# Two halves of a sample's expert lookup: where the dot products and the weighted sums stand between the u and the v stage

## The reference, cut to what matters

```
s        = einsum('thpc,hpkc->thpk', q, keys)            # 8 heads, 2 halves, 128 keys
v1, i1   = top_k(s[:, :, 0], 16);  v2, i2 = top_k(s[:, :, 1], 16)
vals, sel = top_k(v1[..., None] + v2[..., None, :], 16)   # 16 of 16384 experts per head
eid      = e1 * 128 + e2
gate     = softmax(vals)
act      = gelu(einsum('thkd,td->thk', u[eid], h))        # dot products
y        = einsum('thk,thkd->td', gate * act, v[eid])     # weighted sums
```

## Time and profile before

| | |
|---|---|
| median of 3 runs | 2619.02 us (2616.82 to 2620.7) |
| profiled execution | 2623.06 us, of which the span from first to last instruction is 2621.3 us |
| PE busy | 2351.1 us (90%) |
| DVE busy | 1774.2 us (68%) |
| ACT busy | 1396.8 us (53%) |
| POOL busy | 175.5 us (7%) |
| granted TensorE clock, mean | 0.935 |

### The profile page before, as it was taken

How to read it: one execution, slowest core, us unless ns; L and a number is a source line. 1 busy time by engine, 2 the same in 40 slices (tenths; PEclk the granted TensorE clock), 3 DMA queues, 4 the chain that set the end, 5 groups by cost and what they waited for, 6 DMA issues and landing times.

```text
span 2621.3 us, 55587 instructions
## 1 busy us (share of the span) xinstructions
PE 2351.1 (90%) x18004; PEld 2208.7 (84%) x18004; DVE 1774.2 (68%) x4136; ACT 1396.8 (53%) x2867; POOL 175.5 (7%) x185
## 2 busy tenths in 40 slices
PE   6996799999887799999897996899999976999996
PEld 3963699999885599999797875799998966999995
DVE  2435538888757777756555877568888789777654
ACT  2511356666558855555455222466666589555553
POOL 1000000000300012100000000000002200211000
PEclk7985799999999999999988877899999999999998
DMA  7453436555964578855543112346557810887552
GB/s 255 162 171 136 143 129 213 178 184 196 335 208 165 187 234 272 280 178 183 170 136 121 49 56 80 131 156 196 179 182 272 300 45 9 273 276 254 184 184 82
DMA packets 126860, 468.34 MB, mean 179 GB/s; under 512 B 14417, under 2 KB 14577, under 8 KB 125633
## 3 DMA queue, kind: packets, MB, share of 16 engines
q1 hardware_dynamic: 103104, 375.44, 41.7%
q0 software_dynamic: 23680, 92.01, 11.2%
HBM read 456.74 MB, written 10.65 MB: 178 GB/s over the span
## 4 chain that ended last, share of the span: by engine, by line
PE 74%; DVE 9%; ACT 7%; DMA 6%; issue 3%; ACTq 1%; SPq 0%; POOL 0%; DVEq 0%; POOLq 0%
PE ps L1275 21%; PE ps L1276 21%; PE ps L1277 21%; ACT hs L568 5%; DMA big<-in_u_rows,choice 4%; DMA raw<-in_ada_w 2%; PE ps L1304 2%; PE ps L1421 1%; DVE spl L715 1%; PE ps L1437 1%; DVE big L1122 1%; PE ps L1450 1%; ACT hs L581 1%; PE ps L1518 1%; PE ps L1340 1%
## 5 line engine op out<-in xcount | busy, mean ns | idle before, releaser
L1275 PE MATMUL ps<-hs,spl 128*128 128x256 f32 (+1 forms) x4960 | 1425.9, 287 | 88.0 <-DVE hs L767 46.0
L1276 PE MATMUL ps<-hs,spl 128*128 128x256 f32 (+1 forms) x4960 | 1425.9, 287 | 0.0
L1277 PE MATMUL ps<-hs,spl 128*128 128x256 f32 (+1 forms) x4960 | 1421.3, 287 | 0.0
L715 DVE TENSOR_TENSOR spl<-raw,spl 128x512 fp32r<-128x512 f32 x1240 | 839.4, 689 | 554.7 <-ACT spl L449 551.0
L449 ACT ACTIVATE spl<-raw 128x512 fp32r<-128x512 f32 x1240 | 772.4, 630 | 522.8 <-PE ps L1277 522.3
L1275 PEld LDWEIGHTS ps<-hs,spl 128*128 128x128 f32 x4960 | 953.2, 192 | 99.4 <-issue 58.4
L1276 PEld LDWEIGHTS ps<-hs,spl 128*128 128x128 f32 x4960 | 951.8, 192 | 0.0
L1277 PEld LDWEIGHTS ps<-hs,spl 128*128 128x128 f32 x4960 | 948.0, 191 | 0.0
L1518 PE MATMUL ps<-hs,onehot 128*128 128x128 f32 x1024 | 154.5, 298 | 71.7 <-ACT hs L581 61.3
L1518 PEld LDWEIGHTS ps<-hs,onehot 128*128 128x128 f32 x1024 | 131.1, 201 | 100.1 <-ACT hs L581 92.3
L551 ACT ACTIVATE big<-ps 128x256 f32 (+1 forms) x256 | 98.4, 384 | 139.3 <-PE ps L1277 137.8
(11 more groups left out here) (242 smaller groups left out, 1464.9 us busy)
## 6 DMA issues: line engine op xcount, KB each, us to landing
raw<-in_peer_u SPq DMA_DIRECT2D x256, 512.0 KB, 3.7
raw<-in_peer_v SPq DMA_DIRECT2D x256, 512.0 KB, 3.5
raw<-in_ada_w SPq DMA_DIRECT2D x96, 512.0 KB, 5.0
raw<-in_peer_wq SPq DMA_DIRECT2D x32, 512.0 KB, 3.4
raw<-in_hg_w_in SPq DMA_DIRECT2D x32, 512.0 KB, 3.5
raw<-in_ab_w_in SPq DMA_DIRECT2D x28, 512.0 KB, 3.5
raw<-in_ab_w_out SPq DMA_DIRECT2D x8, 512.0 KB, 4.0
big<-in_state_hgrn POOLq DMA_DIRECT2D x8, 512.0 KB, 3.9
```

The source lines that it names most:

```text
L715: dve.tensor_tensor(spl[:, slot % 2, 1, cols], raw[:, slot, cols], spl[:, slot % 2, 0, cols].bitcast(F32), ALU.subtract).then_inc(low_read ...
L1275: pe.matmul(out, spl[:, slot, 0, cols], high, start=start, stop=False, skip_group_check=True)
L1276: pe.matmul(out, spl[:, slot, 0, cols], low, start=False, stop=False, skip_group_check=True)
L1277: return pe.matmul(out, spl[:, slot, 1, cols], high, start=False, stop=stop, skip_group_check=True)
```

## The change

The 32 dot products are divided: the first 16 (EARLY) stay behind the top-k search in the u stage, the other 16 go into groups 0 to 7 of the v stage, one after every second block, at the places where sums stood. The 32 sums move from groups 0 to 15 to groups 10 to 25 (SUM_FROM = 10). With them move their v lookups, the Gelu of the dot products (ACT, now between groups 8 and 9 of the v stage), the multiplication with the softmax gate (DVE, now ahead of group 10), PE's fold (now ahead of group 27) and the read-back of x behind the last v lookup. A dot product in the u stage now brings exactly two feeds. PACE goes from 1450 to 1420.

```
-PACE = 1450
+PACE = 1420
+EARLY = 16
+SUM_FROM = 10
...                                             (ACT, u stage)
-                act.wait_ge(dot_done, PICKS * (l + 1))
-                act.activation(samp_w, samp_w, ACT.Gelu).then_inc(samp_gelu, 1)
...                                             (ACT, v stage)
-                section(act, f"v{l}", expert_out)
+                section(act, f"v{l}", expert_out, groups=(0, SUM_FROM - 1))
+                act.wait_ge(dot_done, PICKS * (l + 1))
+                act.activation(samp_w, samp_w, ACT.Gelu).then_inc(samp_gelu, 1)
+                section(act, f"v{l}", expert_out, groups=(SUM_FROM - 1, EXP // 4))
...                                             (DVE)
+            def dot(l, j):
+                dve.wait_ge(u_landed[j % U_SLOTS], landed(l, j, U_SLOTS))
+                row = fetched[:, j % U_SLOTS, :]
+                dve.tensor_tensor_reduce(row, row, h_rows, 1.0, 0.0, ALU.mult, ALU.add, samp_w[:, j:j + 1]).then_inc(dot_done, 1)
...                                             (DVE, behind the top-k search)
-                for j in range(PICKS):
-                    dve.wait_ge(u_landed[j % U_SLOTS], landed(l, j, U_SLOTS))
-                    row = fetched[:, j % U_SLOTS, :]
-                    dve.tensor_tensor_reduce(row, row, h_rows, ...).then_inc(dot_done, 1)
-                    spent(1230)
+                for j in range(EARLY):
+                    dot(l, j)
+                    spent(2 * PACE)
...                                             (DVE, v stage)
-                dve.wait_ge(samp_gelu, l + 1)
-                link(dve.tensor_tensor(samp_w, samp_w, samp_gate, ALU.mult))
...
-                section(dve, f"v{l}", with_sample, first=True, groups=(0, PICKS // V_SLOTS))
-                section(dve, f"v{l}", expert_out, groups=(PICKS // V_SLOTS, EXP // 4))
+                late = (PICKS - EARLY) // 2
+                for i in range(late):
+                    for s in range(4):
+                        expert_out(i, s)
+                        if s % 2:
+                            dot(l, EARLY + 2 * i + s // 2)
+                section(dve, f"v{l}", expert_out, groups=(late, SUM_FROM))
+                dve.wait_ge(samp_gelu, l + 1)
+                link(dve.tensor_tensor(samp_w, samp_w, samp_gate, ALU.mult))
+                sum_to = SUM_FROM + PICKS // V_SLOTS
+                section(dve, f"v{l}", with_sum, first=True, groups=(SUM_FROM, sum_to))
+                section(dve, f"v{l}", expert_out, groups=(sum_to, EXP // 4))
...                                             (PE, v stage)
-                middle = PICKS // V_SLOTS + 1
+                middle = SUM_FROM + PICKS // V_SLOTS + 1
```

More of the change, by code:

```diff
@@ L1118, in topk @@
                 picked = False
-                for j in range(PICKS):
-                    dve.wait_ge(u_landed[j % U_SLOTS], landed(l, j, U_SLOTS))
-                    row = fetched[:, j % U_SLOTS, :]
-                    dve.tensor_tensor_reduce(row, row, h_rows, 1.0, 0.0, ALU.mult, ALU.add, samp_w[:, j:j + 1]).then_inc(dot_done, 1)
-                    spent(1230)
+                for j in range(EARLY):
+                    dot(l, j)
+                    spent(2 * PACE)
                     if not picked and fed[0] >= topk_row + 4:
@@ L1210, in expert_out, with with_sum @@
                         weight_low(i * 4 + (s + 1), (s + 1) % 2)
-                def with_sample(i, s):
+                def with_sum(i, s):
                     expert_out(i, s)
@@ L1215, in with_sample @@
                         slot = s // 2
-                        dve.wait_ge(v_landed[slot], i * 16 + 16 * (PICKS // V_SLOTS * l + 1))
-                        w = choice[:, 1, bass.ds(i * 2 + (T_PROMPT + slot), 1)]
-                        if isinstance(i, int) and i == 0 and slot == 0:
+                        dve.wait_ge(v_landed[slot], i * 16 + 16 * (PICKS // V_SLOTS * l + 1 - SUM_FROM))
+                        w = choice[:, 1, bass.ds(i * 2 + (T_PROMPT + slot - 2 * SUM_FROM), 1)]
+                        if isinstance(i, int) and slot == 0:
                             ins = dve.tensor_scalar(samp_sum, fetched[:, slot, :], w, None, ALU.mult)
                         else:
-                            dve.wait_ge(sum_done, i * 2 + (PICKS * l + slot))
+                            dve.wait_ge(sum_done, i * 2 + (PICKS * l + slot - 2 * SUM_FROM))
                             ins = dve.scalar_tensor_tensor(out=samp_sum, in0=fetched[:, slot, :], scalar=w, in1=samp_sum, op0=ALU.mult, op1=ALU.add)
                         ins.then_inc(sum_done, 1)
-                section(dve, f"v{l}", with_sample, first=True, groups=(0, PICKS // V_SLOTS))
-                section(dve, f"v{l}", expert_out, groups=(PICKS // V_SLOTS, EXP // 4))
+                late = (PICKS - EARLY) // 2
[10 more added lines that the diff above has]
+                section(dve, f"v{l}", expert_out, groups=(sum_to, EXP // 4))
                 dve.wait_ge(half_done, 2 * (SPLIT[f"v{l}"] + EXP))
```

## The result

The changed kernel takes 2592.96 us in the median of six runs (2585.57 to 2598.87), against 2622.0 us (2616.82 to 2633.19) for the kernel before: ratio 0.9874, 95% interval 0.985 to 0.9898. Forecast were 2591.5 us and a range of 2585 to 2603. The profiled execution took 2592.62 us, 30.4 less than the profiled one before.

What follows compares the result with a forecast made beforehand. PE's matmul pace bounds the kernel, with lookup rounds through three slots stalling it in the dot stretches. 2623.06 - 30.1 + 0.6 = 2593.6 us for the profiled execution; 2591.5 us forecast as a middle with 2589.5, range 2585 to 2603.

Steps and rivals of the forecast that it cites:

- The stall and its size: Dot stretches of both u stages: PE loses 16.3 and 13.8 us to late lookups, together 30.1 us, all of it returning.
- further margin: u stage: beyond 5.8 us of cover left, transfers come at a lower rate than the earlier 319 to 321 GB/s.
- the three longest parts: Lookup round in u: longest dot product, POOL issue and landing come to 11.4 us, against 17.16 us of cover.
- The clock share: Dot stretches: 9.1 of the 30.1 us are matmuls at lower clock behind waits, counted as returning with the idle time.
- The rival (only 21.0 us): Dot stretches: dips have another cause than waits, so only idle time returns, 2600.6 us; chance 0.10.
- The v stage at 0: v stages: sixteen added dot products each and sums moved to groups 10 to 25 cost PE 0.
- Gelu, fold, read-back at 0: v stage: moving Gelu, fold and read-back costs 0; table loads for Gelu would cost at most 2.6 us in all.
- Remains of 0.3 us per layer: Top-k stretch: allowance for remains such as the softmax behind a dot product, 0.6 us in the sum.
- its 1.1 us: Top-k stretch: PE waits only 1.1 us, so PACE 1420 changes between -1.1 and +1.1 per layer, taken as 0.
- The middle between 2589.5 and 2593.6: Whole call: the profile's 4.04 us over the median lie in vanishing waits (2593.6) or elsewhere (2589.5); middle 2591.5 us.

Runs made afterwards that it cites:

- one block per dot product: The changed kernel with one block instead of two behind each of the 16 dot products of the u stage: 2597.63 us, ratio 0.9895.
- the v half alone: Kernel before with Gelu, gate multiplication, v lookups and sums moved to v groups 10 to 25; all 32 dot products stay in u, PACE 1450: 2618.65 us, ratio 0.998.
- three groups of runs: The changed kernel, unaltered, run in three groups, each beside the kernel before: medians 2592.96, 2590.82 and 2593.71 us.
- the run with unwaited lookups: Kernel before, lookups 2 to 32 into slots 0 and 1, dot products reading h_rows and waiting for the first lookup alone: 2592.71 us, ratio 0.9888.
- the one-slot kernel: The changed kernel with one slot for u lookups instead of three: 2627.95 us, ratio 1.0017 to the kernel before.

## Why the prediction was right

**The stall and its size.** Right in both layers: 16.3 and 13.8 us from counting matmuls, 16.6 and 13.9 measured on the u stages. The lookups' round was the cause, as taken from the chain. Without the wait, with DVE's work unchanged and nearly the same traffic, the gain is the same, and three, two and one slots and one block per dot product behave as round against cover says.

The agreement to 0.3 us is partly made: both numbers come from the same profile of the kernel before. In the profile of the v half alone the same stall of layer 1 made a u stage of 385.1 us, which is 20.9 us over the changed kernel's 364.2 and not 13.9. What supports the sum beyond that profile are the medians, which lie 29.0, 30.6 and 31.2 us apart in the three groups of runs.

The prediction named the lower rate of transfers as further margin. It brought the lookups of the u stage nothing: they land in 6.9 us where it was 7.0, and the spacing alone covers them. Also, POOL's issue lies within the landing: in the earlier trace rows the dot product (1.23), 0.28 us and the landing (8.35) make up the round of 9.88. So the 11.4 us of the three longest parts count the issue twice, on the safe side.

**The clock share.** The 9.1 us beyond idle time came back: the two u stages are 30.5 us shorter, 9.5 more than the idle time of 21.0. The rival (only 21.0 us) would have left some 2600.6 us and a clock under 1.00 in the dot stretch; the profile shows 1.00. That the dips follow the waits and not the traffic is shown by the run with unwaited lookups: nearly the same GB/s, no waits, clock 1.00. In that point the rival's own argument was half right: waits do not always bring a dip. One block per dot product had 2.8 and 3.0 us of waits in the two layers, none over 1.1, and full clock. In the one-slot kernel the clock fell to 0.66 behind a wait of 1.8 us, and stayed at 1.00 behind its longest, 2.7 us (between 675 and 685). The slice with the first, and the next two:

```profile
655.00:660.00 5.00, 3.19 (x28) 2.98 (x26) 2.42 (x5) 2.74 (x6) 0.42 (x1) 1.00 0.47 153
660.00:665.00 5.00, 5.00 (x29) 5.00 (x30) 2.28 (x4) 0.89 (x2) 0.73 (x1) 0.66 0.71 216
665.00:670.00 5.00, 5.00 (x45) 5.00 (x43) 2.48 (x5) 4.54 (x7) 1.15 (x1) 1.00 0.64 206
```

The Trainium skill, "TensorE: Matmul & The Clock Gate", section on HAM oscillation, says that waits for DMA that let the clock fall pay the slower clock again each time. The trace agrees for this stall: 9.5 us came back beyond the idle time. But these two kernels show waits that let no clock fall, and in the one-slot kernel the longer wait is one of them, so here the length of a wait did not tell.

**The v stage at 0.** Right. The v half alone measures 0.998 (0.9956 to 1.0005). Layer 1's v stage is 1.4 us longer in the profile after. The rows put that at its start, where the clock is low before the stage's first dot product begins (2195.28): the one-block kernel, with the same v stage, has 364.9 us as before. The first windows of the two, the changed kernel first:

```profile
2185.00:2190.00 5.00, 2.97 (x21) 2.81 (x22) 4.25 (x10) 2.19 (x5) 0.00 (x0) 0.92 0.00 0
2190.00:2195.00 5.00, 5.00 (x34) 5.00 (x34) 1.86 (x5) 1.57 (x3) 0.00 (x0) 0.74 0.30 107
```

```profile
2189.00:2194.00 5.00, 2.97 (x26) 2.81 (x25) 4.29 (x11) 1.77 (x5) 0.00 (x0) 1.00 0.00 0
2194.00:2199.00 5.00, 5.00 (x44) 5.00 (x44) 3.35 (x7) 2.52 (x5) 0.06 (x1) 1.00 0.40 120
```

PE is busy 2.97 us in both first slices, and yet 34 matmuls follow in one and 44 in the other. Whether the change makes such a start more likely stays open: in layer 1 five of the eight profiles with dot products in the v stage have it, all three of the changed kernel among them, and none of the three profiles without. In layer 0 the kernel before has it as well (clock 0.71 from 925 to 930). The prediction also says that groups 10 to 25 held no sums before; groups 10 to 15 did, under the same load per group.

**Gelu, fold, read-back at 0.** Right; no table load came with the Gelu, and the read-back landed in 7.8 to 8.0 us.

**Remains of 0.3 us per layer.** Slightly too much: from 645 to 753 the profile after shows no wait of PE on DVE at all. The top-k stretch keeps its 1.1 us, as assumed.

**The middle between 2589.5 and 2593.6.** A choice between two readings of the profiled run's 4 us, and the three medians (2590.82 to 2593.71) lie on both sides of it. That 2591.5 came out within 1.5 us of the median is in that part luck. The scatter of single runs (11 to 27 us within a group) is wider than that choice, and the traces put most of it ahead of the u stage and into the weigh stage of layer 0, which the change does not touch.

## What to carry to other kernels

Where an in-order engine consumes transfers and also feeds the engine that sets the pace, compare two numbers: the time between two consumptions times the number of slots, and the round of one slot read from the chain. In all kernels here in which the first was larger, no dot product waited. The round is not a constant, though: take it from the stage in question, and expect it to change with the spacing and the slots. Spreading the same consumptions over more of the pacing work gained here what removing the wait altogether gained. Size a stall by counting the pacing engine's instructions against an undisturbed stretch, not by its idle time: a third of this one was clock.

## What was not expected

A lookup of 512 KB has no one landing time. In the u stages it took 7.0 us (median) before, when one was asked for every 2.9 us or so, and 6.9 to 7.1 in the changed kernel, which asks half as often; 8.0 with one block per dot product; and 4.8 with one slot, where no lookup is asked for before the last has landed. In the v stages of the changed kernel it took 4.7 us with all three slots: one is asked for every 5.7 us, so there too each flies alone. What makes the lookups of the u stage slower at nearly the same mean spacing is not shown; what differs in the trace is that there they are issued mostly 4.4 and 7.0 us apart in turn, so that some overlap. A median over both stages hid this, which is why the one-slot kernel lost 40 us and not 93. And two slots would have done.

The granted clock of a stage with many short waits is not fixed by its instructions: the weigh stage of layer 0 ran at 0.83 in one profile and at 0.93 in another of the same kernel, 14 us apart, nearly half of what the change is worth. In a kernel of this kind a difference of a few us is sooner found in the length of the stage that an edit touches than in the time of the call.
